# Multi-head latent attention: queries and keys as plain and rotary tiles, values straight from the projection, scores on halves and quarters of the rows

## The chip, the cores and the metric

The kernel runs on one core of one Trainium2 chip. The metric is the time of one execution on the device in microseconds (us), as the median of several runs. One execution was also profiled; every row below is from it.

## The reference

The reference is one decoder layer on 1,024 tokens of width 1,024 in float32. After a root-mean-square norm one input projection feeds a sparse attention (A), a latent attention (B) and two sigmoid gates. Then come an output projection, an MLP and a gated embedding, each with a residual. The change touches B and its latents:

```python
cq, ckv, kr = split of rmsnorm(x) @ w_in           # 384, 256 and 32 columns
q_b = (rmsnorm(cq) @ w_uq).reshape(1, s, 8, 64 + 32)
q_b = concat([q_b[..., :64], rope(q_b[..., 64:])])
kv  = (rmsnorm(ckv) @ w_ukv).reshape(1, s, 8, 64 + 64)
k_b = concat([kv[..., :64], rope(kr) for all 8 heads]); v_b = kv[..., 64:]
y_b = softmax(causal(q_b @ k_b.T * 96 ** -0.5)) @ v_b
# rope: out = [x1 cos - x2 sin, x2 cos + x1 sin], x1 and x2 the two halves of 16
```

## The kernel before

Activations lie with features on the partitions (rows) and 1,024 tokens on the free axis. Every weight product is made of three passes (high weight by high data, high by low, low by high), in this way: SP loads a slab of 4x256 columns (`w_raw`), ACT rounds it into `w_hi` (L697), POOL subtracts into `w_lo` (L619), and TensorE (PE) multiplies (L1411). Each of the three buffers exists twice: a slab's rounding waits until PE has used the slab two before it (`slab_used`), and its load until POOL is done with that one (`lo_ready`). PSUM has two halves of four banks. Each product, a "group", takes the halves in turn and waits until the half has been emptied (`psum_free`). All queues are in order and written out by hand.

- **Latents.** The projections of `cq` and `ckv` end with `project(((0, P),))`. ACT squares them and POOL adds the squares into `rms_c`; the last addition (L648) raises `c_sum` to 3. A loop of four turns then computes the gates (768 products); ACT puts the gates through the single tile `stage` to DRAM.
- **After the gates** PE sums the squares over the partitions with a matrix of ones (L1495), projects `kr` (96 columns), turns the query norm to columns (L1502), and then works through `LATENT_HEADS`: four groups for the queries of two heads each (`qb`, 96 rows a head: 64 plain and 32 rotary), four for keys and values (`kvb`, keys in rows 0 to 63, values in rows 64 to 127, multiplied by the norm by DVE, L1188), and four that turn the values to tokens on rows (L1518, `vb`). The rotation needs the two halves of 16 rows exchanged, which DMAs do (`swap`), and three DVE operations a head (L1169 to L1171). The rotated `kr` is copied by DMA under the keys of every head.
- **B attention** has 32 steps. A step is a block of 128 queries i and a pair of heads p; its keys are the (i+1)*128 tokens so far. Blocks come as a big and a small one, (4,3), (5,2), (6,1), (7,0), four head pairs each: 16 pairs of steps. For step n PE computes the scores of head e=0 into two banks, adds the causal mask (L1542), then head e=1 into two others. DVE takes each head's row maximum from PSUM (L1235) and a small factor (L1236), ACT the exponential from PSUM (L906, `prob_ready`). The next step's scores of a head wait for that, since they use the same banks. After the scores of n PE turns the probabilities of n-1 (L1573, copied out by ACT L871 and DVE L1204) and multiplies those of n-2 with the values (L1587).
- **A attention** has 32 like steps (scores L1557 on 64 rows, two heads in the two halves of the rows).

## Time and profile before

| | |
|---|---|
| median of 3 runs | 1852.56 us (1852.53 to 1852.88) |
| the profiled execution | 1853.91 us, its span 1852.1 us |
| mean granted clock of PE | 0.974 |
| PE busy | 1751.2 us, 95% of the span |
| DVE, ACT, POOL busy | 46%, 30%, 20% |

The span runs from the first to the last instruction. The rest of an execution's time lies around it. A busy PE is one that has a matmul in it, whatever its rate.

### The profile page before, as it was taken

The numbers are of one execution on the slowest core, as the hardware profiler recorded it, in microseconds if no ns is written. First come the engines' busy times: TensorE is split into PE (matmuls) and PEld (weight loads), VectorE is DVE, ScalarE is ACT, GpSimd is POOL, SyncE is SP. The second block draws the span as 40 slices with busy tenths as digits, with TensorE's granted clock in tenths as the row PEclk, the third lists the DMA queues.
The fourth block names the chain that finished last, engine by engine and source line by source line (L and its number), as shares of the span: only waits on it lengthen the run. The fifth ranks groups of instructions, "written<-read, shape, count | busy, mean of one in ns | idle before, by whom it ended". The sixth has DMA issues, their size and how long they took to land.

```text
span 1852.1 us, 21902 instructions
## 1 busy us (share of the span) xinstructions
PE 1751.2 (95%) x8724; PEld 1381.5 (75%) x8724; DVE 849.3 (46%) x1275; ACT 560.8 (30%) x825; POOL 364.2 (20%) x171
## 2 busy tenths in 40 slices
PE   5899899999799999899998999999999999998996
PEld 4578678877566666678886888888888888886885
DVE  7499999605755566655315212122222122226333
ACT  5421422223255556631222202121121112124113
POOL 2212432222200000212221222222222222222220
PEclk9999999999889999999999999999999999999998
DMA  4202122221200010004420111111111111111112
GB/s 143 57 24 63 29 80 91 91 93 45 74 1 1 1 69 1 2 2 158 160 91 23 46 57 45 45 46 56 45 45 47 55 45 45 48 54 40 40 46 91
DMA packets 82223, 101.70 MB, mean 55 GB/s; under 512 B 5648, under 2 KB 74768, under 8 KB 82160
## 3 DMA queue, kind: packets, MB, share of 16 engines
q1 hardware_dynamic: 79600, 92.17, 16.0%
q10 hardware_dynamic: 2400, 8.65, 1.3%
q8 instruction: 42, 0.69, 0.2%
q0 software_dynamic: 160, 0.02, 0.1%
q14 instruction: 21, 0.17, 0.0%
HBM read 84.97 MB, written 12.85 MB: 53 GB/s over the span
## 4 chain that ended last, share of the span: by engine, by line
PE 85%; DVE 7%; ACT 5%; issue 1%; POOL 1%; DMA 1%; SPq 0%; ACTq 0%; DVEq 0%; POOLq 0%
PE ps L1411 71%; PE ps L1540 4%; PE ps L1573 3%; PE ps L1587 2%; PE ps L1557 2%; DVE prob_a L1243 2%; ACT prob_b L906 1%; PE ps L1652 1%; DVE sc L1117 1%; DVE qb L1170 1%; DVE swap L1169 0%; PE ps L1439 0%; PE ps L1662 0%; PE ps L1702 0%; ACT w_hi L697 0%
## 5 line engine op out<-in xcount | busy, mean ns | idle before, releaser
L619 POOL TENSOR_TENSOR w_lo<-w_raw,w_hi 128x1024 fp32r<-128x1024 f32 x134 | 325.2, 2428 | 1140.9 <-ACT w_hi L697 1140.9
L697 ACT ACTIVATE w_hi<-w_raw 128x1024 fp32r<-128x1024 f32 x134 | 142.0, 1061 | 978.9 <-PE ps L1411 917.5
L1411 PE MATMUL ps<-n_hi,w_hi 128*128 128x512 f32 (+2 forms) x1136 | 356.1, 395 | 17.9 <-POOL w_lo L619 5.2
L1411 PE MATMUL ps<-n_lo,w_hi 128*128 128x512 f32 (+2 forms) x1136 | 353.6, 393 | 0.0
L1411 PE MATMUL ps<-n_hi,w_lo 128*128 128x512 f32 (+2 forms) x1136 | 353.2, 392 | 0.0
L1411 PEld LDWEIGHTS ps<-n_hi,w_hi 128*128 128x128 f32 (+2 forms) x1136 | 214.4, 189 | 67.6 <-POOL w_lo L619 5.0
L1411 PEld LDWEIGHTS ps<-n_lo,w_hi 128*128 128x128 f32 (+2 forms) x1136 | 214.8, 189 | 46.9 <-issue 0.2
L1411 PEld LDWEIGHTS ps<-n_hi,w_lo 128*128 128x128 f32 (+2 forms) x1136 | 214.3, 189 | 46.7
L1339 DVE TENSOR_TENSOR h<-h,ps 128x2048 f32<-128x2048 f32 x32 | 73.2, 2288 | 221.6 <-PE ps L1411 221.6
L1130 DVE TENSOR_SCALAR_CACHE_REDUCE tested<-sc,bar_i 128x384 bf16<-128x384 f32 (+2 forms) x192 | 169.0, 943 | 1.7 <-POOL sc L634 0.6
L1328 DVE SCALAR_TENSOR_TENSOR tmp<-ps,rms 128x1024 f32<-128x1024 f32 x32 | 37.7, 1220 | 266.3 <-PE ps L1411 266.3
L1411 PE MATMUL ps<-hid_hi,w_lo 128*128 128x512 f32 x512 | 157.6, 389 | 0.0
L1411 PE MATMUL ps<-hid_lo,w_hi 128*128 128x512 f32 x512 | 157.6, 389 | 0.0
L1411 PE MATMUL ps<-hid_hi,w_hi 128*128 128x512 f32 x512 | 157.6, 389 | 0.0
L1411 PEld LDWEIGHTS ps<-hid_hi,w_lo 128*128 128x128 f32 x512 | 96.1, 188 | 20.0
L1411 PEld LDWEIGHTS ps<-hid_hi,w_hi 128*128 128x128 f32 x512 | 96.1, 188 | 20.0
L1411 PEld LDWEIGHTS ps<-hid_lo,w_hi 128*128 128x128 f32 x512 | 96.1, 188 | 19.9
L1540 PE MATMUL ps<-kvb,qb 96*128 96x512 f32 (+3 forms) x192 | 80.8, 543 | 6.8 <-issue 4.3
L1235 DVE TENSOR_REDUCE cols<-ps 128x1 f32<-128x640 f32 (+7 forms) x64 | 48.5, 758 | 68.1 <-PE ps L1542 67.4
L1243 DVE CUSTOM_DVE_ANT_0 prob_a<-ps,sc 128x640 f32<-128x640 f32 (+7 forms) x64 | 48.5, 758 | 34.6 <-PE ps L1557 34.3
L1540 PEld LDWEIGHTS ps<-kvb,qb 96*128 96x128 f32 x192 | 33.1, 200 | 37.9 <-issue 26.9
L906 ACT ACTIVATE prob_b<-ps,cols 128x640 f32<-128x640 f32 (+7 forms) x64 | 52.9, 831 | 7.0 <-DVE cols L1236 7.0
(246 smaller groups left out, 2021.2 us busy)
## 6 DMA issues: line engine op xcount, KB each, us to landing
w_raw<-in_w_ff_dram SPq DMA_DIRECT2D x64, 512.0 KB, 3.5
w_raw<-in_w_in_dram SPq DMA_DIRECT2D x28, 512.0 KB, 3.6
gates_scratch<-stage ACTq DMA_DIRECT2D x16, 512.0 KB, 2.7
sig_ab<-gates_scratch SPq DMA_DIRECT2D x8, 1024.0 KB, 5.9
x_tok<-in_x_dram SPq DMA_DIRECT2D x8, 512.0 KB, 10.3
w_raw<-in_w_out_dram SPq DMA_DIRECT2D x8, 512.0 KB, 5.0
xs<-in_x_dram SPq DMA_DIRECT2D x4, 1024.0 KB, 5.4
w_raw<-in_w_ple_gate_dram SPq DMA_DIRECT2D x8, 512.0 KB, 3.4
```

Of the source, the lines that this page charges most:

```text
L619: pool.tensor_tensor(w_lo[s][:, :, :], w_raw[s][:, :, :], w_hi[s][:, :, :].bitcast(F32), ALU.subtract).then_inc(lo_ready, 1)
L697: act.activation(w_hi[s][:, :, :], w_raw[s][:, :, :], ACT.Copy).then_inc(hi_ready, 1)
L906: act.activation(prob_of(n, e)[:, 0:w], src, ACT.Exp, bias=shift_c[:, m % 4:m % 4 + 1], scale=q_norm[:, i:i + 1] if br == "B" else SLOPES[hd],
L1130: ins = dve.tensor_scalar(tested[:, at0:at0 + KEYS[i]], s_i, bar_f[:, f:f + 1], None, ALU.is_ge, ALU.add, accum_out=count_c[:, f:f + 1])
L1235: link(dve.tensor_reduce(top, s, AXIS.X, ALU.max))
L1243: link(dve.tensor_tensor_reduce(prob_of(n, e)[:, 0:w], s, sc[:, SC_AT[i]:SC_AT[i] + w], 1.0, LOWEST, ALU.subtract, ALU.max, top))
L1328: dve.scalar_tensor_tensor(tmp[:, j, t, :], tile_ps(half, t), 0.0, rms[:, :], ALU.max, ALU.mult).then_inc(relu_ready if t == 0 else psum_f ...
L1339: dve.tensor_tensor(pair, pair, bank(4 * half, 4), ALU.add).then_inc(psum_free[half], 1)
L1411: last = pe.matmul(bank(4 * half + 2 * j + t)[0:w, :], wm, xm[:, t * HALF:(t + 1) * HALF], start=(k == 0 and a), stop=(k == total - 1 and ...
L1540: pe.matmul(bank(b + c // HALF)[:, 0:w], qb[0:QB_DIM, hd, q], kvb[0:QB_DIM, hd, c:c + w], start=True, stop=c + w < KEYS[i])
L1557: last = pe.matmul(bank(S_BANK + 2 * e + c // HALF)[:, 0:w], qa[r, p, q], ka[r, p // (PAIRS // KV_HEADS_A), c:c + w], start=True, stop=True)
L1573: last = pe.transpose(bank(u % RING)[:, (k - k0) * P:(k - k0 + 1) * P], prob_of(n, e)[:, k * P:(k + 1) * P], ident[:, :])
```

## The change

The queries become four tiles of plain rows (`qn`, two heads' 64 rows each in the two halves) and two of rotary rows (`qr`, 32 rows for each of four heads). The keys become four plain tiles (`kn`) and one rotary tile `kr` that holds the same 32 rows four times, its weights loaded four times. A product with a permutation `perm` exchanges the halves for rotation (one group for `kr`, one for `qr`), so three rotations of 128 rows replace nine of 32. The values come from products with 128 tokens' latents as the weights and all 512 value columns moving; ACT scales them as it copies. Nine weight slabs replace ten, loaded in pieces of 128 and 256 bytes. The sums of squares and the turned norms move ahead of the gate loop. `qr_other` is `qr` with its halves exchanged, by DMA. A score is now a product on 64 rows, for both heads in turn, and then one on 32 rows: each of the up to four pairs (head, 512 keys) has its own quarter of the rows; the masks of both heads come last. In A the step at which the sums of B are inverted moves by one.

```diff
         VA_GROUP = TT + 6
-        SUM_GROUP = VA_GROUP + 3 + 2 * GATES_N
-        KR_GROUP = SUM_GROUP + 1
-        LATENT_HEADS = [(kind, g) for kind in ("q", "kv", "vt") for g in range(HEADS // 2)]
-        KV_GROUP, UQ_GROUP, VT_GROUP = ([KR_GROUP + 1 + LATENT_HEADS.index((kind, g)) for g in range(HEADS // 2)]
-                                        for kind in ("kv", "q", "vt"))
-        OUT_GROUP = KR_GROUP + 1 + len(LATENT_HEADS) + DT
+        SUM_GROUP = VA_GROUP + 3
...
+        INV_B = NB + 4
         SPREAD_B = [INV_B + 2 + p for p in range(PAIRS)]
...
+            for k0 in range(0, DT, KT):
+                s, _, num, _ = at_.slab()
+                sp.wait_ge(lo_ready, num - 1)
+                for g in range(P // ROPE):
+                    if g == P // ROPE - 1:
+                        sp.wait_ge(kr_w_loaded, 16 * g * (k0 // KT + 1))
+                    sp.dma_start(w_raw[s][:, :, g * ROPE:(g + 1) * ROPE], wt(wi, k0, KT, KR0, ROPE)
+                                 ).then_inc(raw_loaded[s] if g == P // ROPE - 1 else kr_w_loaded, 16)
...
-            def swap_halves(n):
-                if n >= 2:
-                    sp.wait_ge(rope_done, n - 1)
-                b = n % 2
-                sp.dma_start(swap[b][lo:mid, :], ROPES[n][mid:hi, :]).then_inc(swap_loaded[b], 16)
-                sp.dma_start(swap[b][mid:hi, :], ROPES[n][lo:mid, :]).then_inc(swap_loaded[b], 16)
...
+            sp.wait_ge(rope_done, 3)
+            for u in range(2):
+                sp.dma_start(qr_other[HEAD_DIM:P, u, :], qr[0:HEAD_DIM, u, :]).then_inc(qr_copied, 16)
+                sp.dma_start(qr_other[0:HEAD_DIM, u, :], qr[HEAD_DIM:P, u, :]).then_inc(qr_copied, 16)
             load(wt(pb, 0, KT, 0, WCOL))
             load(wt(pa, 0, KT, 0, WCOL))
-            sp.wait_ge(rope_done, 1)
-            for g in range(HEADS // 2):
-                freed(sp, VT_GROUP[g] % 2, free_count(VT_GROUP[g]))
-                for hd in (2 * g, 2 * g + 1):
-                    sp.dma_start(kvb[lo:hi, hd, :], kr[lo:hi, :]).then_inc(kr_copied, 16)
...
             latent(4, tile_ps(half, 0), half)
             latent_hi(4, half)
-            act.wait_ge(c_sum, 3)
+            half = group()
+            act.activation(rms_c[:, 0, :], tile_ps(half, 0), ACT.Sqrt, bias=eps_c, scale=1.0 / QL)
+            act.activation(rms_c[:, 1, :], tile_ps(half, 1), ACT.Sqrt, bias=eps_c, scale=1.0 / KVL).then_inc(
+                psum_free[half], 1)
+            half = group()
+            act.activation(q_norm, tile_ps(half, 0)[:, 0:TT], ACT.Copy, scale=1.0 / SCALE_B)
+            act.activation(kv_norm, tile_ps(half, 0)[:, TT:2 * TT], ACT.Copy).then_inc(psum_free[half], 1)
...
-            half = group()
-            act.activation(rms_c[:, 0, :], tile_ps(half, 0), ACT.Sqrt, bias=eps_c, scale=1.0 / QL)
-            act.activation(rms_c[:, 1, :], tile_ps(half, 1), ACT.Sqrt, bias=eps_c, scale=1.0 / KVL).then_inc(
-                psum_free[half], 1)
+            hi_parts(1, QT)
+            half = group(2)
+            act.activation(kr[:, :], tile_ps(half, 0), ACT.Copy).then_inc(kr_in, 1)
+            act.wait_ge(kr_in, 1)
+            act.sem_inc(psum_free[half], 1)
+            hi_parts(2, QT)
+            half = group(1)
+            act.activation(qr[:, :, :].rearrange("q u n -> q (u n)"), bank(4 * half, 4), ACT.Copy).then_inc(qr_in, 1)
+            act.wait_ge(qr_in, 1)
+            act.sem_inc(psum_free[half], 1)
+            at_.group()
+            for g in range(2):
+                hi_parts(2, QT if g == 0 else 2)
+                half = group(2)
+                act.activation(qn[:, 2 * g:2 * g + 2, :].rearrange("q u n -> q (u n)"), bank(4 * half, 4),
+                               ACT.Copy).then_inc(psum_free[half], 1)
+                at_.group()
+            at_.group()
+            act.wait_ge(kv_inverted, 1)
+            for g in range(2):
+                half = group(2 * g)
+                for j in range(4):
+                    t = 4 * g + j
+                    last = act.activation(vb[:, t, :], bank(4 * half + j), ACT.Copy, scale=kv_norm[:, t:t + 1])
+                last.then_inc(psum_free[half], 1)
             hi_parts(2)
...
-            def rope(n):
-                rows_, sw = ROPES[n][lo:hi, :], swap[n % 2][lo:hi, :]
-                dve.wait_ge(swap_loaded[n % 2], 32 * (n // 2 + 1))
-                link(dve.tensor_tensor(sw, sw, rope_sin[lo:hi, :], ALU.mult))
-                link(dve.tensor_tensor(rows_, rows_, rope_cos[lo:hi, :], ALU.mult))
-                dve.tensor_tensor(rows_, rows_, sw, ALU.add).then_inc(rope_done, 1)
...
-                        last = dve.tensor_tensor(kvb[:, 2 * g + j, :], tile_ps(half, j), rms_c[:, 1, :], ALU.mult)
-                    last.then_inc(psum_free[half], 1)
...
+            link(dve.reciprocal(kv_norm, kv_norm))
+            dve.sem_inc(kv_inverted, 1)
+            link(dve.reciprocal(q_norm, q_norm))
+            dve.wait_ge(gate_saved, 16 * 2 * DT)
+            halves = [m[:, :].rearrange("q (g h j) -> q g h j", h=2, j=half_rope) for m in (perm, ident)]
+            for side in range(2):
+                dve.tensor_copy(halves[0][:, :, side, :], halves[1][:, :, 1 - side, :]).then_inc(perm_ready, 1)
+            def rope(n, half, j):
+                x = kr[:, :] if n == 0 else qr[:, n - 1, :]
+                if n:
+                    dve.wait_ge(rope_done, n)
+                ins = dve.tensor_tensor(rope_t[:, :], tile_ps(half, j), rope_sin[:, :], ALU.mult)
+                if n != 1:
+                    link(ins)
+                    dve.sem_inc(psum_free[half], 1)
                 else:
-                    at_.group()
+                    link(ins)
+                link(dve.tensor_tensor(x, x, rope_cos[:, :], ALU.mult))
+                dve.tensor_tensor(x, x, rope_t[:, :], ALU.add).then_inc(rope_done, 1)
...
-                at_.loop(i, 4, 2, 2)
-                project()
-                project()
-                at_.end(GATES_N)
             half = group()
             pe.wait_ge(c_sum, 3)
             pe.wait_ge(c_sq, QT + KVT)
                     last = pe.matmul(bank(4 * half + 2 * c + t), ones[:, :], rms_c[:, c, t * HALF:(t + 1) * HALF],
                                      start=True, stop=True)
             last.then_inc(turn_done, 1)
+            half = group()
             freed(pe, SUM_GROUP % 2, free_count(SUM_GROUP))
-            for t in range(TT):
-                last = pe.matmul(tile_ps((at_.groups - 1) % 2, 1)[:, t:t + 1], rms_c[0:1, 0, t * P:(t + 1) * P],
-                                 ones[0:1, 0:1], start=True, stop=True)
-            last.then_inc(q_norm_turned, 1)
+            for c in range(2):
+                for t in range(TT):
+                    last = pe.matmul(tile_ps(half, 0)[:, c * TT + t:c * TT + t + 1],
+                                     rms_c[0:1, c, t * P:(t + 1) * P], ones[0:1, 0:1], start=True, stop=True)
+            last.then_inc(turn_done, 1)
+            with pe.Fori(0, GATES_N) as i:
+                at_.loop(i, 4, 2, 2)
+                project()
+                project()
+                at_.end(GATES_N)
...
+            def swap_rows(half, j, x):
+                for t in range(2):
+                    last = pe.matmul(bank(4 * half + 2 * j + t), perm[:, :], x[:, t * HALF:(t + 1) * HALF],
+                                     start=True, stop=True)
+                return last
+            half = group()
+            for k0 in range(2):
+                s, _, num, _ = at_.slab()
+                pe.wait_ge(lo_ready, num + 1)
+                for kk in range(KT):
+                    k = k0 * KT + kk
+                    last = three([bank(4 * half + t) for t in range(2)],
+                                 ((w_hi[s][:, kk, 0:P], w_lo[s][:, kk, 0:P]), normed(k)), k == 0, k == DT - 1)
+                last.then_inc(slab_used, 1)
+            half = group()
             pe.wait_ge(c_lo, QT + KVT)
-            for kind, g in LATENT_HEADS:
+            product(half, FULL, (QT,), lambda k: (cq_hi[:, k, :], cq_lo[:, k, :]))
+            half = group()
+            pe.wait_ge(perm_ready, 2)
+            pe.wait_ge(kr_in, 1)
+            swap_rows(half, 0, kr).then_inc(turn_done, 1)
+            def q_nope():
                 half = group()
-                if kind == "kv":
-                    product(half, FULL, (KVT,), lambda k: (ckv_hi[:, k, :], ckv_lo[:, k, :]))
-                elif kind == "q":
-                    product(half, ((0, QB_DIM), (QB_DIM, QB_DIM)), (QT,),
-                            lambda k: (cq_hi[:, k, :], cq_lo[:, k, :]))
-                else:
...
+            q_nope()
+            half = group()
+            pe.wait_ge(qr_in, 1)
+            for u in range(2):
+                last = swap_rows(half, u, qr[:, u, :])
+            last.then_inc(turn_done, 1)
+            q_nope()
...
+            for g in range(2):
+                half = group()
+                for k in range(KVT):
+                    wh, wl = [w[:, HD:2 * HD] for w in both(kv_slabs[k][0])]
+                    for j in range(4):
+                        tok = slice((4 * g + j) * P, (4 * g + j + 1) * P)
+                        xh, xl = ckv_hi[:, k, tok], ckv_lo[:, k, tok]
+                        for x, w, a, z in ((xh, wh, True, False), (xh, wl, False, False), (xl, wh, False, True)):
+                            last = pe.matmul(bank(4 * half + j), x, w, start=k == 0 and a, stop=k == KVT - 1 and z)
+                    if g == 1:
+                        last.then_inc(slab_used, 1)
+                if g == 0:
                     last.then_inc(turn_done, 1)
...
-            pe.wait_ge(kr_copied, 16 * HEADS)
-            pe.wait_ge(rope_done, HEADS + 1)
+            pe.wait_ge(qr_copied, 64)
+            pe.wait_ge(rope_done, 3)
             def scores_b(n):
                 _, i, p = STEPS[n]
                 q = slice(i * P, (i + 1) * P)
+                chunks = [(c, min(HALF, KEYS[i] - c)) for c in range(0, KEYS[i], HALF)]
+                own, other = (qr, qr_other) if p % 2 == 0 else (qr_other, qr)
+                for c, w in chunks:
+                    for e in range(2):
+                        if c == 0 and n >= 1:
+                            pe.wait_ge(prob_ready, 2 * (n - 1) + e + 1)
+                        r = slice(e * HEAD_DIM, (e + 1) * HEAD_DIM)
+                        pe.matmul(bank(S_BANK + 2 * e + c // HALF)[:, 0:w], qn[r, p, q], kn[r, p, c:c + w],
+                                  start=True, stop=False)
                 for e in range(2):
-                    hd, b = 2 * p + e, S_BANK + 2 * e
-                    if n >= 1:
-                        pe.wait_ge(prob_ready, 2 * (n - 1) + e + 1)
-                    for c in range(0, KEYS[i], HALF):
-                        w = min(HALF, KEYS[i] - c)
-                        pe.matmul(bank(b + c // HALF)[:, 0:w], qb[0:QB_DIM, hd, q], kvb[0:QB_DIM, hd, c:c + w],
-                                  start=True, stop=c + w < KEYS[i])
-                    pe.matmul(bank(b, 2)[:, i * P:(i + 1) * P], ident_b[:, :], causal_b[:, :],
+                    for lower, (c, w) in enumerate(chunks):
+                        r = slice(lower * HEAD_DIM + e * ROPE, lower * HEAD_DIM + (e + 1) * ROPE)
+                        pe.matmul(bank(S_BANK + 2 * e + c // HALF)[:, 0:w],
+                                  (other if lower else own)[r, p // 2, q], kr[r, c:c + w],
+                                  start=False, stop=c + w <= i * P)
+                for e in range(2):
+                    pe.matmul(bank(S_BANK + 2 * e, 2)[:, i * P:(i + 1) * P], ident_b[:, :], causal_b[:, :],
                               start=False, stop=True).then_inc(s_ready, 1)
```

## Rows read from the trace of the kernel before

**Rows 1.** Busy time by stretch: start:end, length, PE, its weight loads, DVE, ACT, POOL, clock, DMA.
```profile
410.70:506.57 95.87, 81.67 (x377) 59.21 (x376) 60.52 (x37) 31.09 (x35) 28.00 (x11) 0.93 0.26 66
506.57:546.91 40.34, 39.13 (x236) 24.36 (x237) 19.40 (x43) 19.60 (x47) 0.00 (x0) 0.84 0.00 1
...
622.93:661.92 38.99, 37.18 (x285) 24.34 (x283) 22.05 (x45) 20.65 (x55) 0.00 (x0) 1.00 0.00 1
705.80:795.00 89.20, 81.79 (x771) 55.93 (x770) 56.86 (x170) 60.34 (x152) 9.44 (x4) 1.00 0.01 1
```

**Rows 2.** Timeline of the scores of block 7, then block 0 (start, length, engine, line).
```profile
632.88 1.99 PE L1540 MATMUL ps<-kvb,qb 96*128 96x512 f32 x4
...
636.59 0.39 PE L1573 MATMUL ps<-ident,prob_b 128*128 128x128 f32 x2
636.79 1.23 DVE L1235 TENSOR_REDUCE cols<-ps 128x1 f32<-128x1024 f32 x1 [0.35 <-PE ps L1542]
...
637.14 1.20 ACT L906 ACTIVATE prob_b<-ps,cols 128x1024 f32<-128x1024 f32 x1
...
638.33 1.20 ACT L906 ACTIVATE prob_b<-ps,cols 128x1024 f32<-128x1024 f32 x1
...
638.81 0.49 PE L1540 MATMUL ps<-kvb,qb 96*128 96x128 f32 x2
...
639.67 0.49 PE L1540 MATMUL ps<-kvb,qb 96*128 96x128 f32 x2 [0.32 <-ACT prob_b L906]
...
642.43 1.98 PE L1540 MATMUL ps<-kvb,qb 96*128 96x512 f32 x4
```

**Rows 3.** Timeline before the gate loop; brackets: idle time before it and what ended it.
```profile
233.61 1.22 PE L1411 MATMUL ps<-n_hi,w_hi 128*128 128x512 f32 x2 [4.56 <-POOL w_lo L619]
...
238.17 2.37 POOL L648 TENSOR_TENSOR rms_c<-rms_c,stage 128x1024 f32<-128x1024 f32 x1
```

**Rows 4.** Groups by line: count, busy us, mean ns, idle before; last, a store's landing.
```profile
L619 POOL TENSOR_TENSOR w_lo<-w_raw,w_hi 128x1024 fp32r<-128x1024 f32 x134 | 325.2, 2428 | 1140.9 <-ACT w_hi L697 1140.9
L697 ACT ACTIVATE w_hi<-w_raw 128x1024 fp32r<-128x1024 f32 x134 | 142.0, 1061 | 978.9 <-PE ps L1411 917.5
...
L1662 PE MATMUL ps<-sq_sum,ones 128*128 128x512 f32 x8 | 7.5, 1094 | 13.3 <-DVE sq_sum L1299 7.2 <-DVE sq_sum L1355 6.2
...
L1502 PE MATMUL ps<-ones,rms_c 1*128 1x1 f32 x16 | 1.9, 246 | 0.0
...
gates_scratch<-stage ACTq DMA_DIRECT2D x16, 512.0 KB, 2.7
```

**Rows 5.** Chain of work that ended last, the MLP (start, length, what).
```profile
1005.72 696.36 PE ps L1411 x3072
```

**Rows 6.** Timeline, PE, late in the latent stage and at the first scores.
```profile
487.99 0.74 PE L1411 MATMUL ps<-ckv_hi,w_hi 128*128 128x512 f32 x2 [2.26 <-DVE kvb L1188]
...
506.57 2.47 PE L1540 MATMUL ps<-kvb,qb 96*128 96x512 f32 x4 [4.28 <-issue]
```

**Rows 7.** Timeline of the scores of block 7 in A, and PE's next line.
```profile
758.48 1.99 PE L1557 MATMUL ps<-ka,qa 64*128 64x512 f32 x8
...
760.40 0.66 PE L1573 MATMUL ps<-ident,prob_a 128*128 128x128 f32 x4
```

**Rows 8.** Timeline of the scores of block 4, then block 3.
```profile
537.57 1.35 PE L1540 MATMUL ps<-kvb,qb 96*128 96x512 f32 x4
...
540.20 0.82 DVE L1235 TENSOR_REDUCE cols<-ps 128x1 f32<-128x640 f32 x1
...
541.20 0.88 ACT L906 ACTIVATE prob_b<-ps,cols 128x640 f32<-128x640 f32 x1
...
542.22 1.12 PE L1540 MATMUL ps<-kvb,qb 96*128 96x512 f32 x2
...
546.64 0.79 ACT L906 ACTIVATE prob_b<-ps,cols 128x512 f32<-128x512 f32 x1
...
546.91 1.34 PE L1540 MATMUL ps<-kvb,qb 96*128 96x512 f32 x3
```

218 lines of the change are left out of this document (113 added, 105 removed).

## The prediction

> **What bounds the kernel now.** I read the table of busy time by stretch first, then timelines of the stretches that the diff touches, because a share of the whole span says nothing about one stage. In the table the reader is to see two stages. From the end of the gate loop to the first score are 95.87 us, in which PE works 81.67 us: this stage has holes. The B attention follows, and there PE works 37.2 of 39.0 us for the last four pairs of steps [rows 1]. So PE sets the pace of B, but only just: the timeline of blocks 7 and 0 shows that the other engines' work fits between PE's own, and that once per pair PE already waits, 0.32 us, for an exponential [rows 2]. The MLP gives the price of a three-pass product: 696.36 us for 3072, 0.2267 us each [rows 5].
>
> **Ahead of the gates.** The sums now stand before the gate loop, and they need the last addition to `rms_c`. Before, PE ended its products at 229.05, waited 4.56 us for a slab and began the gates at 233.61, while POOL ended that addition at 238.17 + 2.37 = 240.55 [rows 3]. Now PE waits until 240.7. Then come 8 float32 passes of 512 columns (a float32 product is two passes, and the rows count passes). With the clock at 2.4 GHz a pass takes about 0.43 us: two heads of block 7 are 8 passes and took 3.7 us with their masks [rows 2]. But the eight of L1662, which stand behind a wait, show 1.094 us each, more than half of the 1.99 that four passes of block 7 show together [rows 2, 4]. So I take the lower level, 1.2 GHz, and 8 x 0.855 = 6.85 (bound below: 3.45). ACT then takes two roots, about 1.06 us each by its 128x1024 copy, plus 0.2 us to react: 2.35. Only then can PE make the 16 small products, 1.95 [rows 4]. All weights for the first gates are ready by then. The gates begin at 240.7 + 6.85 + 2.35 + 0.1 + 1.95 = 251.95, **18.3 us later** (bounds 15 and 19). The loop itself is the same.
>
> **From the gates to the first score.** I follow PE from the end E of the gates. One slab's way through ACT and POOL is 1.06 + 2.43 + 0.15 = about 3.65 us [rows 4], and it begins when PE has left the slab two before.
> - `kr`, 48 products, 10.9: E to 11.0. The next slab's rounding stands behind ACT's last two gate tiles on `stage`, each 1.0 us and a store of 2.7 that ACT waits for, with some 0.2 between [rows 4]. With a rounding before them they end at E+9.0, and the slab is ready at 12.5. Rotary queries, 36 products, 8.2: to 20.85. Turning `kr`, 4 passes: to 22.6.
> - ACT is in order: it rounds a slab that PE frees at 20.85 (to 22.1) before it copies `qr` (two 1.0 us pieces, to 24.1), and the first plain queries need that PSUM half. Hole of 1.6. Two tiles of 18 products, 4.1 each: to 32.5. Turning `qr`, 8 passes: 36.0. Two more tiles: 44.3.
> - Plain keys need both last slabs, and the second can be rounded only when the last query slab is free: hole of 3.7, to 48.0. Then four groups of 24 products, 5.5 each: to 70.0. ACT's last four value copies of 512 columns, about 0.6 each: the first score at E+72.5.
>
> The removed exchange DMAs, the eight copies of `kr` and the nine narrow rotations cost nothing more to leave out: they filled the old holes (2.26 us before 487.99, 4.28 us before 506.57 [rows 6]). The three new rotations lie under the plain products. If this cover went, each would cost its three DVE operations, about 1.2 us as the maximum over as many columns [rows 2]. The small DMA pieces are nowhere in this trace; they have 7 us or more to land, so I take zero; a slab 3 us late would cost 3, and twice that is my bound. Three holes will bring some half clock, as after the 2.26 us hole; I add 2. So 74.5 in place of 95.9: **21.4 us less** (bounds 15 and 23.4).
>
> **The B stage.** *Scores of one step.* Before, a head of block 7 is four passes of 512 columns, both heads 3.71 us to the next line [rows 2]. In A two heads on 64 rows each run side by side: 8 records in 1.92 us [rows 7]. Now the plain part takes that, the rotary part one quarter each, at best 0.855 us for all four, plus two more changes of the row split (A's row leaves about 0.1 us each) and two masks: about 3.05. That is 0.66 less for block 7, 0.5, 0.3 and 0.0 for 6, 5, 4, and 0.0 to 0.2 more for the small ones. By PE's work alone the stage wins about 5.8 us.
>
> *What the new order adds.* Both heads' scores are now ready only at the end of all products, at T, because the rotary part and the masks close both. Before, head 0's maximum ran while PE made head 1's scores. From T: maximum of head 0 1.23, factor, maximum of head 1, factor, exponential of head 1, 1.20, release: 0.25 + 1.56 + 1.23 + 0.3 + 1.20 + 0.1 = about 4.5 us. Before it was 639.67 - 636.59 = 3.1 [rows 2]. PE fills 2.25 of it (636.59 to 638.81) with turning and values, as before. Then it waits, because the plain products of head 1 need that exponential and everything else stands behind them in PE's queue. Block 0's scores end at T+5.2 in place of T+3.45: **1.75 more**. After them the big block's turning and a little value work take 2.4, but the small block's second exponential comes at 2.9: 0.45 more. Pair (7,0): +1.75 + 0.45 - 0.66 = +1.55.
>
> Pair (4,3): from T, 0.2 + 0.98 + 0.82 + 0.3 + 0.88 + 0.1 = 3.3 until head 1 is free, against PE's 2.2 of other work (about 540.0 to 542.22). Block 3's scores end at T+5.45 in place of 4.2: +1.25. Then the chain to its second exponential, 3.35 (ACT also copies the turned block 4 in between), against 2.7 before: +0.65 [rows 8]. Sum +1.9. The two pairs between come by the same sum to 1.5 and 1.7. Mean 1.67, times 16: **+27 us**. Below, with free changes of the split, 20; above, if the quarters run only two by two, +8.5 to 35.
>
> At its start the old stage ran at a mean clock of 0.84 and its first four pairs took 40.3 us, 3 more than 4 x 9.34 [rows 1, 8]. The new one follows straight on full products; I take **1.5 us less** (0 to 3). The A stage, output and MLP keep their work; the moved inversion of the sums waits for nothing that is not done.
>
> The Trainium skill ("TensorEngine Tiling (Array Packing)", Tiling Modes, Key Properties) says that changing the tiling mode drains TensorE. A's rows show its passes until 760.47 and the next line at 760.40 [rows 7], so a full drain is not seen; with one, each of the 64 new changes would cost 0.07 us more and the sum would be 4.5 us higher.
>
> **Sum.** +18.3 - 21.4 + 27 - 1.5 = +22.4 on a span of 1852.1 gives 1874.5. The profiled execution lies 1.8 above its span and 1.35 above the median: 1853.91 + 22.4 - 1.35 = **1875 us**.
>
> **The rivals.**
> - *B follows PE's work (faster).* If the exponentials did not hold PE, B would win 5.8 us and the time be 1852.6 + 18.3 - 21.4 - 1.5 - 5.8 = 1842. For it speaks that PE is busy 95% of this stage [rows 1]; against it, that the wait exists already at 0.32 us [rows 2]. It decides by whether head 1's exponential comes within PE's 2.25 us of other work. Chance 0.08.
> - *The quarters run one after another.* Then the rotary part costs 2 x (all keys), 39 us more in all: 1914. A shows only two at once [rows 7]. Chance 0.07. The Trainium skill ("TensorEngine Tiling (Array Packing)", Theoretical Speedup) gives up to 4x for 32 rows, which speaks against this rival.
> - *The clock.* With holes of 1 to 2 us in every step PE's clock may fall. A has holes of 0.6 and kept 1.00 [rows 1]. One stretch of 3.4 us at half rate a pair costs 1.7: 16 x 1.7 on top, 1902. Chance 0.05.
> - *Terms cancel*, B's growth under 6 us: no change. Chance 0.04.
>
> **The numbers.** The forecast, 1875, has 0.76. The bounds add up to 1860 (15 - 23.4 + 20 - 3 is +8.6) and 1895 (19 - 15 + 35 + 4 is +43). This leaves out about 2 in 10. A change within 0.2% (3.7 us) is what a measurement of this kernel cannot tell from none. Faster 0.08, same 0.04, slower 0.88.
>
> **What would show it.** Gates beginning near 252; first score near 252 + 177 + 74.5 = 503.5; pairs of B steps near 11 us in place of 9.4 with PE waiting for `prob_b` before both blocks' scores; DVE's maxima of both heads back to back. Pairs of 9 us, or rotary passes that start one after another, would prove me wrong.

## The result: 1883.3 us in place of 1852.7

The changed kernel takes 1883.3 us (median of 4 runs, 1882.48 to 1884.21), the kernel before 1852.72 (1852.53 to 1853.73, measured beside it). The ratio is 1.0164, 95% interval 1.0146 to 1.0182, so the change costs 30.6 us. The forecast was 1875 with a range of 1860 to 1895. The profiled executions differ by 28.6 us of span, and the stages account for that:

| stage | before, us | after, us | difference | forecast |
|---|---|---|---|---|
| to the first gate product | 233.61 | 254.93 | +21.3 | +18.3 |
| gate loop | 177.09 | 175.77 | -1.3 | 0 |
| end of gates to first score | 95.87 | 74.55 | -21.3 | -21.4 |
| B attention | 155.35 | 187.88 | +32.5 | +27 - 1.5 |
| A attention to the end | 1190.2 | 1187.6 | -2.6 | 0 |

The gate loop has the same work in both; before, 6.2 us of it ran at half clock (a granted clock of 0.50, 233.6 to 239.8), after 3.3 us (254.9 to 258.2), and half of that difference is about 1.4 us.

**Ahead of the gates.** This is PE's timeline of the kernel after; it answers to [rows 3], where the gates began at 233.61.

```profile
239.67 6.07 PE L1507 MATMUL ps<-rms_c,ones 128*128 128x512 f32 x8 [11.51 <-POOL rms_c L653]
...
248.04 6.96 PE L1515 MATMUL ps<-ones,rms_c 1*128 1x1 f32 x32 [2.30 <-ACT rms_c L818]
...
254.93 1.22 PE L1429 MATMUL ps<-n_hi,w_hi 128*128 128x512 f32 x2
```

PE waits 11.51 us for POOL's last addition. It then makes the eight passes of the sums, waits 2.30 us for the two roots, and makes the 16 small products, which are 32 passes.

**The latent stage and B.** The table of busy time by stretch, columns as in [rows 1]:

```profile
254.93:430.70 175.77, 175.77 (x770) 145.43 (x770) 104.87 (x167) 40.48 (x39) 39.31 (x15) 0.99 0.29 89
430.70:505.25 74.55, 64.85 (x266) 50.23 (x264) 18.35 (x15) 21.62 (x23) 20.11 (x8) 0.98 0.26 67
505.25:548.00 42.75, 39.76 (x252) 21.14 (x252) 16.15 (x37) 21.26 (x45) 4.65 (x2) 0.92 0.00 1
548.00:595.00 47.00, 44.59 (x337) 26.85 (x336) 19.67 (x44) 22.05 (x52) 0.00 (x0) 0.96 0.01 1
595.00:645.00 50.00, 45.56 (x359) 29.52 (x356) 22.25 (x50) 23.68 (x57) 0.00 (x0) 0.93 0.00 1
645.00:693.13 48.13, 41.36 (x336) 27.73 (x332) 21.51 (x45) 22.27 (x56) 0.00 (x0) 0.93 0.01 1
```

The second row is the latent stage: 9.7 us of holes (idle time of PE) in 74.55, where before there were 14.2 in 95.87. The last row is the end of B, in which PE works 41.36 of 48.13 us; before it was 37.18 of 38.99 [rows 1].

**One pair of B.** The timeline of the scores of block 7 and then block 0, which answers to [rows 2]:

```profile
658.20 2.16 PE L1622 MATMUL ps<-kn,qn 64*128 64x512 f32 x8
...
660.29 0.69 PE L1628 MATMUL ps<-kr,qr_other 32*128 32x512 f32 x1
660.30 0.18 PEld L1628 LDWEIGHTS ps<-kr,qr 32*128 32x128 f32 x1
660.30 0.69 PE L1628 MATMUL ps<-kr,qr 32*128 32x512 f32 x1
660.30 0.18 PEld L1628 LDWEIGHTS ps<-kr,qr_other 32*128 32x128 f32 x1
660.31 0.69 PE L1628 MATMUL ps<-kr,qr_other 32*128 32x512 f32 x1
660.31 0.18 PEld L1628 LDWEIGHTS ps<-kr,qr 32*128 32x128 f32 x1
660.31 0.69 PE L1628 MATMUL ps<-kr,qr 32*128 32x512 f32 x1
...
660.83 0.59 PE L1628 MATMUL ps<-kr,qr_other 32*128 32x512 f32 x1
...
661.37 0.28 PE L1632 MATMUL ps<-causal_b,ident_b 128*128 128x128 bf16 x2
...
661.63 1.22 DVE L1252 TENSOR_REDUCE cols<-ps 128x1 f32<-128x1024 f32 x1 [3.15 <-PE ps L1632]
...
663.02 1.22 DVE L1252 TENSOR_REDUCE cols<-ps 128x1 f32<-128x1024 f32 x1
663.14 1.20 ACT L912 ACTIVATE prob_b<-ps,cols 128x1024 f32<-128x1024 f32 x1 [1.00 <-DVE cols L1253]
...
664.49 0.48 PE L1622 MATMUL ps<-kn,qn 64*128 64x128 f32 x2 [0.72 <-ACT prob_b L912]
664.52 1.20 ACT L912 ACTIVATE prob_b<-ps,cols 128x1024 f32<-128x1024 f32 x1
...
665.87 0.48 PE L1622 MATMUL ps<-kn,qn 64*128 64x128 f32 x2 [0.89 <-ACT prob_b L912]
666.28 0.30 PEld L1628 LDWEIGHTS ps<-kr,qr_other 32*128 32x128 f32 x4
...
666.71 0.28 PE L1632 MATMUL ps<-causal_b,ident_b 128*128 128x128 bf16 x2
```

The reader is to see four things. The rotary passes of both heads and both halves of the keys start within 0.02 us of each other, so the four quarters of the rows do work at once. A round of them takes 0.53 us. The two maxima stand back to back from 661.63. And PE waits for each of the two exponentials, 0.72 and 0.89 us, ahead of block 0; before there was one wait of 0.32 [rows 2].

### The profile page after: what moved, and what is told of

The parts are those of the page before. It is cut to its first block, busy times and chain, and to the rows that moved or that the text cites. A ratio compares the mean times of both kernels' runs of the same rounds, so it can differ in the third digit from the quotient of the medians.

```text
span 1880.7 us, 22134 instructions
## 1 busy us (share of the span) xinstructions
PE 1763.8 (94%) x8844; PEld 1385.6 (74%) x8844; DVE 809.8 (43%) x1256; ACT 562.4 (30%) x820; POOL 361.6 (19%) x170
## 3 DMA queue, kind: packets, MB, share of 16 engines
q10 hardware_dynamic: 2592, 9.44, 1.3%
## 4 chain that ended last, share of the span: by engine, by line
PE 87%; DVE 6%; ACT 4%; POOL 1%; issue 1%; DMA 0%; ACTq 0%; DVEq 0%; POOLq 0%
PE ps L1429 70%; PE ps L1663 3%; PE ps L1622 3%; PE ps L1647 2%; PE ps L1677 2%; PE ps L1628 2%; PE ps L1530 2%; DVE prob_a L1260 1%; DVE cols L1252 1%; ACT prob_b L912 1%; PE ps L1742 1%; DVE sc L1123 1%; PE ps L1598 1%; POOL w_lo L624 1%; PE ps L1457 0%
## 5 line engine op out<-in xcount | busy, mean ns | idle before, releaser
L1429 PE MATMUL ps<-n_hi,w_hi 128*128 128x512 f32 (+1 forms) x1120 | 349.5, 394 | 9.6 <-ACT cq L783 4.2
L1429 PE MATMUL ps<-n_lo,w_hi 128*128 128x512 f32 (+1 forms) x1120 | 347.5, 392 | 0.0
L1429 PE MATMUL ps<-n_hi,w_lo 128*128 128x512 f32 (+1 forms) x1120 | 347.4, 392 | 0.0
L1429 PEld LDWEIGHTS ps<-n_hi,w_hi 128*128 128x128 f32 (+1 forms) x1120 | 211.4, 189 | 56.7 <-ACT cq L783 4.4
L1429 PEld LDWEIGHTS ps<-n_lo,w_hi 128*128 128x128 f32 (+1 forms) x1120 | 211.2, 189 | 45.3
L1429 PEld LDWEIGHTS ps<-n_hi,w_lo 128*128 128x128 f32 (+1 forms) x1120 | 211.1, 189 | 45.2
L1622 PE MATMUL ps<-kn,qn 64*128 64x512 f32 (+3 forms) x192 | 59.6, 531 | 17.2 <-ACT prob_b L912 14.6
L674 POOL TENSOR_TENSOR yb_lo<-yb,yb_hi 128x1024 fp32r<-128x1024 f32 x4 | 9.4, 2360 | 288.5 <-ACT yb_hi L922 288.5
L1622 PEld LDWEIGHTS ps<-kn,qn 64*128 64x128 f32 x192 | 26.2, 191 | 40.9 <-ACT prob_b L912 29.7
```

Source lines behind the costliest of these rows:

```text
L1429: last = pe.matmul(bank(4 * half + 2 * j + t)[0:w, :], wm, xm[:, t * HALF:(t + 1) * HALF], start=(k == 0 and a), stop=(k == total - 1 and ...
L1622: pe.matmul(bank(S_BANK + 2 * e + c // HALF)[:, 0:w], qn[r, p, q], kn[r, p, c:c + w], start=True, stop=False)
```

## The experiments

To compare B stages, the table below gives the shortest time from the second mask of one pair's small block to that of the next pair, between two pairs of the same blocks, read off PE's timeline of each kernel. The shortest is taken because some pairs hold a stretch of half clock. The kernels of e3 and e8 have the pairs of the kernel after.

| kernel | (4,3) | (5,2) | (6,1) | (7,0) | time, us |
|---|---|---|---|---|---|
| before | 9.35 | 9.34 | 9.44 | 9.54 | 1852.7 |
| after | 11.31 | 11.26 | 11.21 | 11.22 | 1883.3 |
| e1 masks last | 9.42 | 9.89 | 10.36 | 10.84 | 1865.1 |
| e4 no rotary part | 9.19 | 9.35 | 9.51 | 9.73 | 1851.3 |
| e5 masks last, both waits | 10.94 | 11.09 | 11.25 | 11.47 | 1885.4 |
| e6 short maxima, new | 11.15 | 10.72 | 10.29 | 10.09 | 1867.5 |
| e12 short maxima and exponentials | 9.65 | 9.43 | 9.21 | 9.06 | 1847.6 |
| e11 old scores on 64 rows | 10.03 | 9.92 | 9.89 | 9.99 | 1861.7 |
| e2, e9, e10 new latents, old scores | 9.25 | 9.34 | 9.44 | 9.54 | 1847.1, 1837.1, 1847.0 |
| e7 short maxima, old | 9.25 | 9.34 | 9.44 | 9.54 | 1850.2 |

The 9.25 of the last two lines is the second pair of the stage, which in the kernel before held half clock (9.92); their next two pairs take 9.35 to 9.40, against 9.35.

**e1: masks last.** The theory is that B loses by the order in which scores become ready, not by PE's work. First that order alone, in the kernel before.

```diff
-                    pe.matmul(bank(b, 2)[:, i * P:(i + 1) * P], ident_b[:, :], causal_b[:, :],
+                for e in range(2):
+                    pe.matmul(bank(S_BANK + 2 * e, 2)[:, i * P:(i + 1) * P], ident_b[:, :], causal_b[:, :],
```

> The kernel before with one move: the causal masks of both heads come after the products of both heads, so both heads' scores are ready only at the end. PE's work is the same. If the order of readiness is what the B stage lost by (my step: both maxima start at T), each pair of steps grows by 1.4 to 1.9 us and the time is 1852.7 + 27 = 1880 (1873 to 1886). If the loss came from the split into halves and quarters (changes of the split, more passes, clock), nothing of it is in this kernel and the time stays within 3 us of 1853.

Measured: 1865.11 us (1864.51 to 1865.32), ratio 1.0070 (1.0053 to 1.0087). That is +12.8, under half of what was expected. The order costs something, and more the longer the maxima are, but not all. What differs from the kernel after is where PE waits: here head 0's products still start before head 1's exponential is done. Run e5 takes that up.

**e2: the old scores on the new latents.** The rotary products go; each head has one product of 96 rows per 512 keys, as before, but on rows of its neighbour, so the scores are not right and only the time counts.

```diff
-                for c, w in chunks:
-                    for e in range(2):
...
+                for e in range(2):
...
+                    if n >= 1:
+                        pe.wait_ge(prob_ready, 2 * (n - 1) + e + 1)
+                    for c in range(0, KEYS[i], HALF):
+                        w = min(HALF, KEYS[i] - c)
+                        pe.matmul(bank(b + c // HALF)[:, 0:w], qn[0:QB_DIM, p, q], kn[0:QB_DIM, p, c:c + w],
...
```

> The changed kernel with its score products alone put back: 96 rows for each head in turn, mask behind each head (the rows are those of the plain tiles, so the scores are not those of the reference: the rotary part is left out and a head takes rows of its neighbour). If the whole loss of the B stage lies in the new scores, the stage goes back from 187.9 to about 155.5 us and the time to 1851 (1847 to 1855). If a part lies in the new layout of values and probabilities, or in what the latent stage leaves behind, the time stays above 1860.

Measured: 1847.06 us (1846.05 to 1848.29), ratio 0.9973 (0.9962 to 0.9985), and pairs as before the change. So all of the loss in B comes with the new scores, and the new latents by themselves, with the sums in front of the gates, win 5 us.

**e3: the sums behind the gates.** In the kernel after, the sums, the roots and the small products move back behind the gate loop.

```diff
-        SUM_GROUP = VA_GROUP + 3
-        NORM_GROUP = SUM_GROUP + 1
-        KR_GROUP = NORM_GROUP + 1 + 2 * GATES_N
+        SUM_GROUP = VA_GROUP + 3 + 2 * GATES_N
+        KR_GROUP = SUM_GROUP + 1
+        NORM_GROUP = KR_GROUP + 1
...
```

> The changed kernel with the sums of squares and the turned norms behind the gate loop again (sums, then kr, then norms, then the rotary queries). If the wait for the last addition and the roots and small products ahead of the gates are a real cost, the gates begin at 233.6 again (21.4 us earlier) and about 6 us come back behind the gates, because ACT's roots come before the next weight rounding and the norms take 3.7: 1883.3 - 15 = 1868 (1864 to 1872). If the work only moves, without the wait counting, the time stays at 1880 to 1884.

Measured: 1873.67 us (1869.74 to 1875.08), ratio 1.0119 (1.0102 to 1.0135), 9.6 less than after. PE's timeline behind the gate loop:

```profile
409.64 3.59 PE L1515 MATMUL ps<-rms_c,ones 128*128 128x512 f32 x8
415.75 0.73 PE L1524 MATMUL ps<-n_hi,w_hi 128*128 128x512 f32 x2 [2.51 <-ACT stage L826]
...
426.85 3.73 PE L1550 MATMUL ps<-ones,rms_c 1*128 1x1 f32 x32
```

The same eight and 32 passes cost 3.59 and 3.73 us here, where the granted clock is full, against 6.07 and 6.96 ahead of the gates. The gates begin at 234.09, 20.8 us earlier. Behind them these passes and a wait of 2.51 us for ACT's last gate tile come back, 9.8 together, where about 6 had been expected: B's first maximum comes 10.8 us earlier (497.05 against 507.86), and not 15.

**e4: no rotary part.** The rotary products of the kernel after are left out.

```diff
-                for e in range(2):
-                    for lower, (c, w) in enumerate(chunks):
-                        r = slice(lower * HEAD_DIM + e * ROPE, lower * HEAD_DIM + (e + 1) * ROPE)
...
```

> The changed kernel without the rotary products of the scores (the scores lack their rotary part; all else as it is). If the rotary passes and the two changes of the split lie wholly on the path (they stand before both heads' readiness), a big step loses 1.2 us and a small one 0.4 to 1.1: 16 pairs x 1.9 = 30 us less, 1853, and the waits for the exponentials stay. If they are hidden under the waits for the exponentials, less than 10 us less, above 1873.

Measured: 1851.34 us (1846.39 to 1852.88), 32 less than after, 2.0 us a pair. In the kernel after the rotary passes of block 7 last 1.08 us (660.29 to 661.37) and those of block 0 last 0.43 (666.28 to the masks at 666.71), 1.51 together. The pair (7,0) shrinks by 1.49. For blocks 4 and 3 they are 1.07 and 1.06, and that pair shrinks by 2.12. So the whole length of these passes lies on what sets the pace of B; none of it is hidden behind a wait. e4 still has the waits for the exponentials (0.71 and 0.89 us ahead of block 0), so it does not tell yet whether the passes cost time by themselves or because they stand in one line with those waits; e12 does.

**e5: masks last and both waits in front.** e1, with one wait moved.

```diff
+                if n >= 1:
+                    pe.wait_ge(prob_ready, 2 * (n - 1) + 2)
                 for e in range(2):
                     hd, b = 2 * p + e, S_BANK + 2 * e
-                    if n >= 1:
-                        pe.wait_ge(prob_ready, 2 * (n - 1) + e + 1)
...
```

> The kernel before, with its own 96-row scores, but the masks of both heads behind both heads' products, and PE waits for both exponentials of the step before ahead of the first product. It is e1 (+12.8 us) with one more thing, the wait for head 1's exponential moved ahead of head 0's products. Theory: the new kernel loses in B because scores of both heads, maxima, factors and exponentials form one serial chain, in which nothing of a step's scores can run beside the step before; then this kernel loses what the new one loses and a little more, since its scores of block 7 take 3.7 us in place of the 3.2 that the new one's take: pairs of 11.2 to 11.8 us, +30 us (22 to 36). Rival: the new kernel's loss beyond e1 comes from the rotary passes (row split changes, the pace of passes on 32 rows); then the moved wait adds little: pairs as in e1 (9.4 to 10.8), +13 to +17 us.

Measured: 1885.39 us (1883.33 to 1886.5), ratio 1.0174 (1.0159 to 1.0190). The kernel before, with its own products, loses as much as the change does, 32.3 us against the kernel before measured beside it; its pairs, 10.94 to 11.47, are near the 11.21 to 11.31 of the kernel after. The timeline of its block 7 and block 0:

```profile
671.16 3.70 PE L1540 MATMUL ps<-kvb,qb 96*128 96x512 f32 x8 [0.33 <-ACT prob_b L906]
674.70 0.28 PE L1543 MATMUL ps<-causal_b,ident_b 128*128 128x128 bf16 x2
...
674.96 1.23 DVE L1235 TENSOR_REDUCE cols<-ps 128x1 f32<-128x1024 f32 x1 [3.70 <-PE ps L1543]
...
677.85 1.20 ACT L906 ACTIVATE prob_b<-ps,cols 128x1024 f32<-128x1024 f32 x1
...
679.20 0.71 PE L1540 MATMUL ps<-kvb,qb 96*128 96x128 f32 x4 [2.10 <-ACT prob_b L906]
```

From the masks at 674.70 to the end of head 1's exponential at 679.05 are 4.35 us, and PE has 2.4 of other work in them. It waits 2.10.

**e6 and e7: maxima over 128 keys.** The exponent is scaled by 1/8 as well, so that it stays small. The results are not right, and only the time counts.

```diff
-                        link(dve.tensor_reduce(top, s, AXIS.X, ALU.max))
+                        link(dve.tensor_reduce(top, bank(S_BANK + 2 * e)[:, 0:P], AXIS.X, ALU.max))
```

> The kernel after, with the maxima of the B scores taken over the first 128 keys alone (the exponent is scaled down by 8 so that it stays small), so that a maximum of block 7 takes about 0.3 us in place of 1.22. PE's work is the same. Theory (serial chain): a pair loses nearly all that the two maxima of the big block and of the small one of 512 to 128 keys lose: (7,0) 2 x 0.95, (6,1) 2 x 0.85, (5,2) 2 x 0.75, (4,3) 2 x (0.5 + 0.4); about 1.7 a pair, 27 us in all, until PE's own work bounds it (pairs of about 9.3): 1858 (1853 to 1865). Rival (PE's own new work, split changes and slower passes set the pace): 1 to 6 us less than after, 1877 to 1882.

> The same edit of the maxima in the kernel before. There PE waits once in a pair, 0.32 us, for an exponential. Theory: PE's work bounds it, so it gains only these waits, 16 x 0.1 to 0.35: 1 to 6 us, 1847 to 1851. Rival (the chain through maximum and exponential binds the kernel before too): 12 us or more less, 1840 or under.

Measured: 1867.53 us (1865.84 to 1869.12) for the new kernel, 15.8 less than after; 1850.18 (1848.07 to 1852.33) for the old one, 2.9 less than the kernel before beside it.

The second number is the one expected, but not for the reason given: the waits that e7 was to remove are all there. Its pairs are those of the kernel before to 0.01 us, but for the second one. In its timeline:

```profile
634.42 0.22 PE L1542 MATMUL ps<-causal_b,ident_b 128*128 128x128 bf16 x1
...
634.86 0.28 ACT L871 ACTIVATE prob_tb<-ps 128x128 f32<-128x128 f32 x1 [3.69 <-PE ps L1573]
635.03 1.20 ACT L906 ACTIVATE prob_b<-ps,cols 128x1024 f32<-128x1024 f32 x1
...
637.56 0.49 PE L1540 MATMUL ps<-kvb,qb 96*128 96x128 f32 x2 [0.32 <-ACT prob_b L906]
```

ACT's first exponential begins 0.61 us behind head 1's mask, as before the edit (636.53 and 637.14 there), although its maximum was done long before: in ACT's queue it stands behind the copy of turned probabilities (L871). So the maxima did not bind the old kernel; the order of ACT's work did, for 0.32 us. The profiled execution of e7 is 2.8 us shorter; 1.0 of it lies ahead of the gates (232.62 against 233.61), which the edit does not touch, and 1.1 from there to the third pair of B, with 3.4 us less at half clock at B's start.

e6 lies between the theory (1858) and the rival (1877 to 1882), and the table by stretch shows why it was undecided. The first two rows are four pairs each, up to the small block of the first pair (6,1) and of the first pair (7,0); the third is the last three pairs (7,0):

```profile
559.46:602.33 42.87, 41.75 (x335) 25.39 (x335) 12.22 (x44) 20.88 (x52) 0.00 (x0) 1.00 0.01 1
602.33:643.48 41.15, 39.75 (x333) 25.20 (x334) 12.76 (x44) 20.50 (x52) 0.00 (x0) 1.00 0.01 2
643.48:673.76 30.28, 28.61 (x252) 19.02 (x252) 10.24 (x33) 15.44 (x39) 0.00 (x0) 1.00 0.00 1
```

PE seems busy 97% of the first, so it looked as if PE's own work had grown by 1.2 us a pair (before it was 36.94 us in the same four pairs). The timeline of block 3, the small one of its pair, with ACT's exponential of head 1, tells otherwise:

```profile
545.11 0.88 ACT L912 ACTIVATE prob_b<-ps,cols 128x640 f32<-128x640 f32 x1
...
545.27 1.99 PE L1622 MATMUL ps<-kn,qn 64*128 64x512 f32 x4
547.19 0.70 PE L1628 MATMUL ps<-kr,qr_other 32*128 32x512 f32 x2
```

Four passes, two for each head, took 1.92 us. The two rounds of rotary passes behind them, of as many columns, took 1.06. By PE's own records head 1's first pass started 0.87 us after head 0's (546.14 and 545.27), when its exponential had ended (it began at 545.11 and lasted 0.88). The rotary products need both heads, so PE waited, beneath passes of head 0 that the records count as work. Run e12 tests that.

**e12: short exponentials too.** e6, with the exponentials over 128 keys.

```diff
-                        m, hd, w = 2 * n + e, 2 * p + e, KEYS[i]
+                        m, hd, w = 2 * n + e, 2 * p + e, P if br == "B" else KEYS[i]
```

> The kernel after with the short maxima of e6, and with the exponentials of B taken over the first 128 keys alone as well (0.45 us each in place of 0.56 to 1.20; the rest of each row of prob_b is left as it was, and the row sums count those 128 alone). PE's products are those of the kernel after. In e6 the pairs still took 10.1 to 11.1 us, and PE showed as busy: there the plain products of head 1 start up to 0.87 us after those of head 0, since they wait for its exponential, and the rotary products wait for both, so a wait hides beneath head 0's passes. Theory (all of the loss in B is the chain from the scores through maxima and exponentials to head 1's scores; the new scores are not more work for PE): with the exponentials short too the chain ends before PE's other work does, pairs of 8.9 to 9.4 us, 1847 (1843 to 1853). Rival (part of e6's long pairs is PE's own: the changes of the row split and passes on few rows): pairs stay at 9.8 to 10.8, 1858 to 1867.

Measured: 1847.58 us (1844.58 to 1852.39), ratio 0.9975 (0.9964 to 0.9986). The same stretches as above, with PE's products those of the kernel after:

```profile
553.07:590.65 37.58, 36.85 (x333) 23.67 (x334) 12.20 (x44) 15.57 (x52) 0.00 (x0) 1.00 0.01 2
590.65:627.31 36.66, 36.36 (x335) 24.41 (x335) 12.74 (x44) 14.94 (x52) 0.00 (x0) 1.00 0.01 2
627.31:654.49 27.18, 27.18 (x251) 18.16 (x252) 10.24 (x33) 11.30 (x39) 0.00 (x0) 1.00 0.00 1
```

PE now never waits in the last stretch, and a pair (7,0) takes 9.06 us. Pairs of 9.06 to 9.65 rule the rival out (9.8 to 10.8): with maxima and exponentials short, B loses nothing, so its loss is the chain from scores to exponentials. The pairs differ from those before by +0.31 to -0.48 us. That is not PE's work alone, for no run shortens the exponentials of the kernel before: its pair (7,0) still holds the wait of 0.32. PE's busy time in the last stretch, 9.06 us a pair, was 9.30 before (27.90 in three).

**e8: only the small products behind the gates.**

```diff
-        NORM_GROUP = SUM_GROUP + 1
-        KR_GROUP = NORM_GROUP + 1 + 2 * GATES_N
+        NORM_GROUP = SUM_GROUP + 1 + 2 * GATES_N
+        KR_GROUP = NORM_GROUP + 1
...
```

> The kernel after, in which the sums of the squares and the roots stay ahead of the gate loop, and only the 16 small float32 products on one row each (32 passes, 6.96 us at 1.2 GHz) and their copies go behind it, ahead of the rotary key. There the clock is at 2.4 GHz and they take about 3.7 us. Theory (the 6.96 us lie whole on PE's path): the gates begin 9 us earlier (that is the 6.96 and the wait for the root's last piece), the stage behind the gates is 3.7 us longer: 5.5 us less (4 to 7), 1877.8. Rival (the slab rounding behind the gates hides them, since PE waits there for the rotary key's slab): up to 7 to 9 us less. Rival 2: the earlier gates meet an unready slab and gain under 3 us.

Measured: 1883.11 us (1880.85 to 1883.68), 0.2 less than after: a miss. PE's timeline:

```profile
245.74 1.02 PE L1430 MATMUL ps<-n_hi,w_hi 128*128 128x512 f32 x2
...
420.36 4.48 PE L1522 MATMUL ps<-ones,rms_c 1*128 1x1 f32 x32
...
426.46 1.22 PE L1531 MATMUL ps<-n_hi,w_hi 128*128 128x512 f32 x2 [1.62 <-ACT stage L830]
```

The gates begin 9.19 us earlier, as expected, but behind them 4.48 and a wait of 1.62 come in front of the rotary key, and the first maximum of B is 3.5 us earlier (504.33 against 507.86). Of those 3.5 only 1.9 are left at the last maximum (689.09 against 690.97): in this execution the half clock at the start of B lasts 20.5 us, in that of the kernel after 6.8. From there to the end this execution takes 3.1 us more, with one more stretch of half clock (723.5 to 726.9). Where such a stretch falls is not something that this edit controls, and what it would be worth without it stays open.

**e11: the old scores on 64 of 96 rows.** The kernel before, the rotary rows left out.

```diff
-                        pe.matmul(bank(b + c // HALF)[:, 0:w], qb[0:QB_DIM, hd, q], kvb[0:QB_DIM, hd, c:c + w],
+                        pe.matmul(bank(b + c // HALF)[:, 0:w], qb[0:NOPE, hd, q], kvb[0:NOPE, hd, c:c + w],
```

> The kernel before, its B scores with the first 64 of their 96 rows alone (the rotary part is left out), head after head in the same order, so that two passes never run side by side. In the kernel after, and in the run with short maxima, passes of 512 columns on 64 or 32 rows are issued 0.53 us apart, those on 96 and 128 rows 0.43. Theory (a pass on fewer rows is slower by itself): 8 passes of block 7 and 4 short ones of block 0 cost 0.1 and 0.03 us more each; about 0.9 us a pair, the pairs of 9.34 to 9.55 become 10.2 to 10.5, and the time is 12 to 16 us longer. Rival (the pace falls because passes run side by side): no change, 1850 to 1854.

Measured: 1861.72 us (1860.80 to 1866.36), ratio 1.0055 (1.0039 to 1.0070): +9.3, between the two. The timeline of a head of block 7:

```profile
654.96 1.98 PE L1540 MATMUL ps<-kvb,qb 64*128 64x512 f32 x4
656.87 0.23 PE L1542 MATMUL ps<-causal_b,ident_b 128*128 128x128 bf16 x1
```

Four passes take 1.92 us to the mask. Four on 96 rows took 1.82 before (632.88 [rows 2] to the mask at 634.70). In PE's own records the passes on 64 rows start at 654.959, 655.492, 655.921 and 656.350, and the mask at 656.872: 0.53, 0.43, 0.43, 0.52. On 96 rows (e5, 671.16 to 674.70) only the first is 0.53 and the last is 0.43. So a pass on few rows is not slower. What costs about 0.1 us stands between the last pass on 64 rows and the mask on 128. Four heads a pair give 0.4 by that, and pairs grow by 0.44 to 0.69; the 0.69 of (4,3) is not explained. Neither theory had this.

**e9 and e10: new latents with old scores.** Each head gets one tile of 96 rows again. For the odd heads the plain rows are copied down by DMA, and the rotary rows of queries and keys are copied in. The new latent stage stays. e9 also has the sums behind the gates, as e3.

```diff
+            for g in range(2):
+                sp.wait_ge(qn_in, g + 1)
+                sp.dma_start(qo[0:NOPE, 2 * g:2 * g + 2, :], qn[NOPE:P, 2 * g:2 * g + 2, :]).then_inc(q_out, 16)
...
+                sp.wait_ge(kn_in, g + 1)
+                sp.dma_start(ko[0:NOPE, 2 * g:2 * g + 2, :], kn[NOPE:P, 2 * g:2 * g + 2, :]).then_inc(k_out, 16)
...
+                    for c in range(0, KEYS[i], HALF):
+                        w = min(HALF, KEYS[i] - c)
+                        pe.matmul(bank(b + c // HALF)[:, 0:w], qs[0:QB_DIM, p, q], ks[0:QB_DIM, p, c:c + w],
...
```

> A version that takes from the change what the runs showed to be worth something: the new latents (plain and rotary tiles, the permutation product, values with tokens on rows) with the sums, roots and norm products behind the gate loop, but the scores as in the kernel before, head after head on 96 rows. For it the odd heads' plain rows and the rotary rows are brought by DMA, behind the last slab loads on SP's queue, to rows 0 to 95 of one tile a head, about 4 MB inside the chip's memory of the core. Theory: e2 (1847.06) less what the late sums gave in e3 (9.6) is 1837.5 (1833 to 1843), if the copies have landed by the first score, and pairs of steps as before. Rival: the copies of the keys begin only when the key tiles are written, some 22 and 17 us ahead of the first score, and 2 MB of them take longer than that: PE then waits ahead of the first score, 5 to 15 us, and nothing is won on the kernel before.

> The same with the sums, roots and norm products ahead of the gate loop, as in the kernel after: it is e2 with right operands and their copies. Theory (the copies are hidden): as e2, 1847 (1845 to 1850). Rival (copies late): 1852 or more.

Measured: e9 1837.11 us (1835.86 to 1838.85), ratio 0.9915 (0.9901 to 0.9928), faster than both kernels. e10 1847.03 us (1844.59 to 1848.66), ratio 0.9969 (0.9957 to 0.9981), the same as e2, so the copies are hidden; in e9 the last of them landed at 494.26, 3.4 us ahead of the first score. PE's timeline of e9 at both ends of the latent stage:

```profile
411.20 3.59 PE L1540 MATMUL ps<-rms_c,ones 128*128 128x512 f32 x8
...
497.66 1.35 PE L1649 MATMUL ps<-kn,qn 96*128 96x512 f32 x4 [2.51 <-ACT vb L894]
```

From the gates to the first score are 86.5 us against 95.87 [rows 1], and what PE waits for last is ACT's copy of the values, not a DMA. The next 6.84 us, to the first pair's second mask, were 8.97 before.

## Why the prediction was right, and where not

The forecast of 1875 was 8 us low, inside its range, and its mechanism held. On the span the miss is 6.2 us: +3.0 ahead of the gates and +7.0 in B, less 1.3 in the gate loop and 2.6 in A and behind it. That the last two took 3.9 us back was luck. The other 2 us are how the profiled executions lie to the medians. By the prediction's own steps:

- **Ahead of the gates, +18.3; measured +21.3.** The wait for POOL's addition ended at 239.67 (240.7 foreseen), the sums took 6.07 (6.85), the roots 2.30 (2.45). The term that was mis-sized is the 16 small products: 1.95 was taken, 6.96 measured. The row it was read from [rows 4] counts 16 records, eight products of two passes, at full clock; here are 32, at half clock (340 ns and more each, against 245 in e3). Half clock had been taken for the sums, and not for the products right behind a further wait. The wait and the sums came out 1.8 us short, which hid part of the 5.0.
- **Gates to first score, 74.5; measured 74.55.** The holes foreseen were 1.5, 1.6 and 3.7 us, and 2.5 ahead of the first score. The trace has 2.03 ahead of the rotary queries, 1.30 ahead of the first plain query tiles, 3.87 ahead of the keys and 2.51 ahead of the first score, and one stretch of half clock (480.0 to 483.4), 1.7 where 2 were taken. The small DMA pieces cost nothing that can be seen.
- **B, pairs +1.9 to +1.55, mean 1.67; measured +1.97, +1.92, +1.77, +1.67** without half clock, 29.3 us for 16 pairs where 27 were foreseen. The chain from T was right in each part: maxima at 0.26 and 1.65 us after the mask, exponential of head 1 over at 4.35 and PE's product behind it at 4.50 (about 4.5 foreseen; its terms as written add up to 4.64). e5 shows that this order and this wait alone, with the old products, cost as much; e12 shows that with short maxima and exponentials nothing is lost. The stage's +32.5 is 27.4 for the 15 steps from pair to pair, 0.85 at the start, and the rest, some 4 us net, is mostly half clock.
- **The wait in front of head 1 matters more than the masks.** The prediction gave one chain its whole price. e1 against e5 divides it: masks last costs 12.8 us, the wait in front of both heads 20.3 more.
- **PE's work, -5.8 for the stage; measured about -1.3 at most.** By e12 the pairs are worth +0.31, +0.09, -0.23 and -0.48 us, four of each, and of the -0.48 the wait of 0.32 that e12 lacks is a part. The rotary part of block 7 took 1.08 us (660.29 to 661.37) and not 0.855. Here a reading failed: the prediction took from [rows 7] that a full drain at a change of the row split is not seen, because passes seemed to last past the next line's start. The ends of passes are modelled, and their starts show the change: 0.53 for the first and last pass of a group and 0.43 between. The Trainium skill ("TensorEngine Tiling (Array Packing)", Tiling Modes, Key Properties) says that changing the mode drains the engine. These rows agree: 0.52 from the last start to the next line, against 0.43 on 96 rows. With the 4.5 us that the prediction worked out for such a drain the sum would have been 1879.5.
- **Start of B, -1.5.** It did not come: to the second mask of the first pair it took 9.82 us, before 8.97, though the half clock there lasted 6.8 us in place of 20.5.
- **The clock.** This rival, with 0.05, came true in part. The mid-B stretches of the kernel after have a granted clock of 0.93 to 0.96 (last column but two of the table by stretch), with five stretches of 3.4 us at half clock, and the pairs that hold one are 0.7 to 1.5 us longer: about 5 us. Before, it was 1.00 in the last four pairs [rows 1].
- **The quarters one after another** (1914): excluded by the four starts within 0.02 us, as **B follows PE's work** (1842) is by the waits of 0.72 and 0.89. Where they are taken away, in e12, the time is 1847.6.
- **A to the end, 0; measured -2.6.** From the first to the last score pass of A it is 127.25 us before and 125.00 after. Before, one stretch of 3.4 us (686.9 to 690.3) ran at half clock there, after none. But the runs on the kernel before without such a stretch (e1, e5, e7, e11) also take 125.8 to 126.0, and those on the kernel after (all but e8) 125.0 to 125.4, so 0.4 us or more belongs to the changed code, most likely the moved inversion of the sums. No run tests that.
